# Two-layer hybrid encoder with top-2-of-8 experts: weights stored in tiles of one piece per partition, and two of twelve half loads of the few-token experts multiplied whole in plain fp32

## What is computed

```python
def swiglu(h, w1, w3, w2):
    return (jax.nn.silu(h @ w1) * (h @ w3)) @ w2

def moe_ffn(h, router, w1, w3, w2):
    ...
    logits = (t @ router).astype(jnp.float32)
    top_v, top_i = lax.top_k(logits, TOP_K)
    top_w = jax.nn.softmax(top_v, axis=-1)
    gates = jnp.sum(jax.nn.one_hot(top_i, N_EXPERTS, dtype=jnp.float32) * top_w[..., None], axis=1)
    out = jnp.zeros_like(t)
    for e in range(N_EXPERTS):
        out = out + gates[:, e:e + 1] * swiglu(t, w1[e], w3[e], w2[e])
```

## Time and profile before

| | before |
|---|---|
| median of 3 executions | 1627.55 us |
| lowest, highest | 1626.26, 1627.86 us |
| profiled execution, its own time | 1627.98 us |
| its span, first to last instruction | 1626.3 us |
| mean granted TensorE clock | 0.981 of 2.4 GHz |
| busy: PE, DVE, ACT, POOL | 1546.5, 1302.4, 1101.7, 30.5 us |
| mean DMA rate over the span | 283 GB/s |
| read from HBM | 457.96 MB |

### The profile page before, as it was taken

The page is one execution under the profiler, slowest core; times in us unless marked ns, Lnnn a source line. Parts: engine busy times, 40 slices in busy tenths (PEclk is TensorE's granted clock), DMA queues, the critical chain, the costliest instruction groups (busy, mean ns, idle before and its releaser), DMA issues.

```text
span 1626.3 us, 22748 instructions
## 1 busy us (share of the span) xinstructions
PE 1546.5 (95%) x8636; PEld 1311.1 (81%) x8636; DVE 1302.4 (80%) x1455; ACT 1101.7 (68%) x1299; POOL 30.5 (2%) x37
## 2 busy tenths in 40 slices
PE   7999999999999997999999988999998999898998
PEld 7999869999899984788888766888666788666786
DVE  4887745554688774789888999988999989999986
ACT  4775343333567523677777978878888778888785
POOL 3000000000000003000000000000000000000000
PEclk9999999999999998999999999999999999999999
DMA  9555356555455539699999999999999999999990
GB/s 261 179 162 181 105 185 195 185 186 182 138 174 159 179 112 381 252 357 356 362 346 351 371 371 374 392 359 357 367 375 372 392 356 344 382 364 383 390 362 26
DMA packets 231400, 460.55 MB, mean 283 GB/s; under 512 B 7434, under 2 KB 79478, under 8 KB 231286
## 3 DMA queue, kind: packets, MB, share of 16 engines
q1 hardware_dynamic: 230262, 457.22, 79.1%
q0 software_dynamic: 832, 1.74, 0.7%
q10 hardware_dynamic: 192, 0.08, 0.0%
HBM read 457.96 MB, written 1.05 MB: 282 GB/s over the span
## 4 chain that ended last, share of the span: by engine, by line
PE 71%; DVE 20%; ACT 6%; DMA 2%; issue 2%; ACTq 0%; SPq 0%; DVEq 0%
DVE w_lo L583 13%; PE bank L996 11%; PE bank L997 11%; PE bank L1000 11%; PE bank L739 8%; PE bank L740 8%; PE bank L741 8%; PE bank L784 3%; ACT w_hi L577 2%; PE bank L974 2%; DMA ring<-in_w_in 2%; PE bank L977 2%; PE bank L1031 1%; DVE w_lo L543 1%; ACT w_hi L535 1%
## 5 line engine op out<-in xcount | busy, mean ns | idle before, releaser
L583 DVE TENSOR_TENSOR w_lo<-arena,w_hi 128x1024 fp32r<-128x1024 f32 x486 | 574.0, 1220 | 54.6 <-ACT w_hi L577 46.7
L577 ACT ACTIVATE w_hi<-arena 128x1024 fp32r<-128x1024 f32 x492 | 503.9, 1056 | 114.1 <-PE bank L1000 88.6
L543 DVE TENSOR_TENSOR w_lo<-ring,w_hi 128x2048 fp32r<-128x2048 f32 x89 | 203.7, 2290 | 153.2 <-ACT w_hi L535 152.1
L739 PE MATMUL bank<-h_hi,w_hi 128*128 128x256 f32 x992 | 284.4, 287 | 4.3 <-DVE w_lo L543 2.6
L740 PE MATMUL bank<-h_lo,w_hi 128*128 128x256 f32 x992 | 282.1, 284 | 0.0
L741 PE MATMUL bank<-h_hi,w_lo 128*128 128x256 f32 x992 | 282.0, 284 | 0.0
L535 ACT ACTIVATE w_hi<-ring 128x2048 fp32r<-128x2048 f32 x89 | 170.2, 1914 | 123.1 <-PE bank L741 80.8
L583 DVE TENSOR_TENSOR w_lo<-ring,w_hi 128x1024 fp32r<-128x1024 f32 x180 | 213.3, 1220 | 19.4 <-ACT w_hi L577 16.9
L996 PE MATMUL bank<-w_hi,h_hi 128*128 128x512 f32 x560 | 224.2, 400 | 2.0 <-DVE h_lo L1912 2.0
L997 PE MATMUL bank<-w_hi,h_lo 128*128 128x512 f32 x560 | 218.8, 391 | 0.0
L577 ACT ACTIVATE w_hi<-ring 128x1024 fp32r<-128x1024 f32 x180 | 185.3, 1056 | 34.1 <-PE bank L1000 31.4
(11 more groups left out here) (281 smaller groups left out, 2111.6 us busy)
## 6 DMA issues: line engine op xcount, KB each, us to landing
arena<-in_moe_w SPq DMA_DIRECT2D x246, 1024.0 KB, 7.0
ring<-in_moe_w SPq DMA_DIRECT2D x90, 1024.0 KB, 6.9
ring<-in_ffn_w SPq DMA_DIRECT2D x33, 1024.0 KB, 5.3
ring<-in_w_gate SPq DMA_DIRECT2D x32, 1024.0 KB, 5.3
ring<-in_w_in SPq DMA_DIRECT2D x16, 1024.0 KB, 6.4
ring<-in_w_branch SPq DMA_DIRECT2D x8, 1024.0 KB, 4.9
ring<-in_w_out SPq DMA_DIRECT2D x8, 1024.0 KB, 4.9
x_tok<-in_x SPq DMA_DIRECT2D x2, 512.0 KB, 4.1
```

The lines of the kernel that those rows point to most:

```text
L543: nc.vector.tensor_tensor(w_lo[:, m % LO, :], raw, w_hi[:, m % HI, :].bitcast(F32), ALU.subtract)\
L577: nc.scalar.activation(half_hi[:, m % AHEAD, :], raw_of(n)[:, HALF * (m % 2):HALF * (m % 2) + HALF], ACT.Copy)\
L583: eng.tensor_tensor(half_lo[:, m % AHEAD, :], raw_of(m // 2)[:, HALF * (m % 2):HALF * (m % 2) + HALF], half_hi[:, m % AHEAD, :].bitcast(F3 ...
L739: pe.matmul(out_, a[0], b[0], start=start, stop=False)
```

## The change

Three things change. The ten large weights are stored in another order (`in_tiles`), in which the 1 MB of a unit or load is one stretch of memory with 8 KB per partition, so `drams` and `expert_drams` return it directly, and a DMA has one piece per partition. In a few-token expert, the third half of h1 and of h3 (q = 2, the k-tiles 4 and 5) is no longer split: `half_whole` multiplies the raw fp32 weight with an unsplit fp32 copy of the tokens (`h_few`, 64 columns), in two plain fp32 matmuls of 512 columns; ScalarE makes `h_few` once per such expert. And the splits are numbered by rank among the halves that are split, so buffers and the six-ahead distance count only these; SyncE waits for such a half to be used (`half_used`) instead of for its lo part. The `all_tokens` branch still splits every half.

```diff
--- before.py
+++ after.py
@@ -46,6 +46,9 @@
 AHEAD = 6
 SMALL = (2, 4, 6)
 FEW = 64
+WHOLE_Q = 2
+LAST_Q = 3
+FEW_K = 2 * WHOLE_Q - 4
...
+        self.whole = {self.first[(kind, i, 0)] + WHOLE_Q for kind in ("h1", "h3") for i in range(STEPS) if i // S_MOE in SMALL}
+        self.split = [m for m in range(self.halves) if m not in self.whole]
+        self.rank = {m: r for r, m in enumerate(self.split)}
...
+        h_few = mix(2, FEW)
...
-        def split_half_hi(m):
+        def split_half_hi(m, r, prior):
 
             n = m // 2
             nc.scalar.wait_ge(raw_loaded[n % RAW], 16 * (n // RAW + 1))
-            if m >= AHEAD:
-                nc.scalar.wait_ge(half_used, m - AHEAD + 1)
-            nc.scalar.activation(half_hi[:, m % AHEAD, :], raw_of(n)[:, HALF * (m % 2):HALF * (m % 2) + HALF], ACT.Copy)\
+            if prior is not None:
+                nc.scalar.wait_ge(half_used, prior + 1)
+            nc.scalar.activation(half_hi[:, r % AHEAD, :], raw_of(n)[:, HALF * (m % 2):HALF * (m % 2) + HALF], ACT.Copy)\
                 .then_inc(half_hi_done, 1)
 
-        def split_half_lo(eng, m):
-            eng.wait_ge(half_hi_done, m + 1)
-            eng.tensor_tensor(half_lo[:, m % AHEAD, :], raw_of(m // 2)[:, HALF * (m % 2):HALF * (m % 2) + HALF],
-                              half_hi[:, m % AHEAD, :].bitcast(F32), ALU.subtract)\
-                .then_inc(half_lo_pool if ex.by_pool(m) else half_lo_dve, 1)
+        def split_half_lo(eng, m, r, halves=1):
+            eng.wait_ge(half_hi_done, r + 1)
+            eng.tensor_tensor(half_lo[:, r % AHEAD, :], raw_of(m // 2)[:, HALF * (m % 2):HALF * (m % 2) + HALF],
+                              half_hi[:, r % AHEAD, :].bitcast(F32), ALU.subtract)\
+                .then_inc(half_lo_pool if ex.by_pool(m) else half_lo_dve, halves)
...
             if kind == "in":
                 _, l, w = key
-                return w_in[l].rearrange("(k p) c -> p k c", p=P)[:, :, IN_COL[w]:IN_COL[w] + US]
+                return w_in[l, 0, IN_COL[w] // US]
...
             if kind == "w2":
-                rows = MU * s + 2 * P * j
-                return w[at, rows:rows + 2 * P, :].rearrange("o (k p) d -> p (o k) d", p=P)
-            rows = D // 2 * j
-            return w[at, rows:rows + D // 2, MU * s:MU * s + MU].rearrange("o (k p) f -> p (o k) f", p=P)
+                return moe_w2[0, at, 2 * s + j, 0].rearrange("o p c -> p (o c)")
+            return {"h1": moe_w1, "h3": moe_w3}[kind][0, at, j, s].rearrange("o p c -> p (o c)")
...
                 j = n % RAW
                 if n >= RAW:
                     for m in (2 * (n - RAW), 2 * (n - RAW) + 1):
-                        wait_half_lo(sp, m)
+                        if m in ex.whole:
+                            sp.wait_ge(half_used, m + 1)
+                        else:
+                            wait_half_lo(sp, m)
...
-                src = expert_drams(key, expert)
-                sp.dma_start(raw_of(n).rearrange("p (k c) -> p k c", k=src.shape[1]), src).then_inc(raw_loaded[j], 16)
+                sp.dma_start(raw_of(n), expert_drams(key, expert)).then_inc(raw_loaded[j], 16)
...
             def half_few(m, outs, first, final):
 
-                pe.wait_ge(half_hi_done, m + 1)
-                w, wl = half_hi[:, m % AHEAD, :], half_lo[:, m % AHEAD, :]
+                r = ex.rank[m]
+                pe.wait_ge(half_hi_done, r + 1)
+                w, wl = half_hi[:, r % AHEAD, :], half_lo[:, r % AHEAD, :]
                 for x, (both, cols, dst) in enumerate(outs):
...
+            def half_whole(m, outs):
+                n = m // 2
+                pe.wait_ge(raw_loaded[n % RAW], 16 * (n // RAW + 1))
+                w = raw_of(n)[:, HALF * (m % 2):HALF * (m % 2) + HALF]
+                for whole, cols, dst in outs:
+                    last = pe.matmul(dst, whole, w[:, cols], start=False, stop=False, skip_group_check=True)
+                last.then_inc(half_used, 1)
             def inner_few(kind, i, toks, b):
                 for q in range(4):
+                    m = ex.first[(kind, i, 0)] + q
+                    if m in ex.whole:
+                        half_whole(m, [(h_few[:, k, :], slice(MU * k, MU * k + MU), bank[b][0:FEW, :]) for k in range(2)])
+                        continue
                     outs = [(h_hi[:, 2 * q + k, toks], slice(MU * k, MU * k + MU), bank[b][:, :]) for k in range(2)]
-                    half_few(ex.first[(kind, i, 0)] + q, outs, lambda x: q == 0 and x == 0, lambda x: q == 3 and x == 1)
+                    half_few(m, outs, lambda x: q == 0 and x == 0, lambda x: q == LAST_Q and x == 1)
...
             def next_hi(u):
+                if u in ex.rank and ex.rank[u] + AHEAD < len(ex.split):
+                    r = ex.rank[u] + AHEAD
+                    split_half_hi(ex.split[r], r, u)
+            def next_hi_all(u):
                 if u + AHEAD < ex.halves:
...
+                if e in SMALL and c == 1:
+                    fn(h_few, bank[b][:, :].rearrange("p (k n) -> p k n", k=4)[:, FEW_K:FEW_K + 2, 0:FEW], ACT.Copy)
...
             def next_lo(u):
-                m = u + AHEAD
-                if m < ex.halves and not ex.by_pool(m):
-                    split_half_lo(dve, m)
+                if u in ex.rank and ex.rank[u] + AHEAD < len(ex.split):
+                    r = ex.rank[u] + AHEAD
+                    split_half_lo(dve, ex.split[r], r, ex.split[r] - ex.split[r - 1])
...
+TILES = {"w_in": (D, US), "w_gate": (D, US), "w_branch": (US, D), "w_out": (US, D), "ffn_w1": (D, US), "ffn_w3": (D, US),
+         "ffn_w2": (US, D), "moe_w1": (D // 2, MU), "moe_w3": (D // 2, MU), "moe_w2": (2 * P, D)}
+def in_tiles(a, rows, cols):
+    lead, (r, c) = a.shape[:-2], a.shape[-2:]
+    n = len(lead)
+    a = a.reshape(*lead, r // rows, rows // P, P, c // cols, cols)
+    a = a.transpose(*range(n), n, n + 3, n + 2, n + 1, n + 4)
+    return a.reshape(*lead, r // rows, c // cols, P, rows // P * cols)
...
-        a = np.ascontiguousarray(inputs[name])
+        a = np.ascontiguousarray(in_tiles(inputs[name], *TILES[name]) if name in TILES else inputs[name])
```

More of the change, by code:

```diff
@@ L989, in outer_few, with half @@
                     half_few(ex.first[("w2", i, 0)] + c, outs, lambda x: first and c == 0, lambda x: final and c == 3)
[L991 to L994 removed]
+            def half(m, r, outs, first, final):
+                pe.wait_ge(half_hi_done, r + 1)
+                w, wl = half_hi[:, r % AHEAD, :], half_lo[:, r % AHEAD, :]
                 for x, (hi, lo, cols, dst) in enumerate(outs):
@@ L1007, in inner, with outer @@
                             for toks, b in tiles for k in range(2)]
-                    half(ex.first[(kind, i, 0)] + q, outs, lambda x: q == 0 and x % 2 == 0, lambda x: q == 3 and x % 2 == 1)
-            def outer(i, acts):
+                    m = ex.first[(kind, i, 0)] + q
+                    half(m, rank(m), outs, lambda x: q == 0 and x % 2 == 0, lambda x: q == 3 and x % 2 == 1)
+            def outer(i, acts, rank):
                 first, final = i % S_MOE == 0, i % S_MOE == S_MOE - 1
@@ L1014, in outer @@
                     outs = [(hi, lo, slice(512 * n, 512 * n + 512), bank[b + n][:, :]) for hi, lo, b in acts(c) for n in range(2)]
-                    half(ex.first[("w2", i, 0)] + c, outs, lambda x: first and c == 0, lambda x: final and c == 3)
+                    m = ex.first[("w2", i, 0)] + c
+                    half(m, rank(m), outs, lambda x: first and c == 0, lambda x: final and c == 3)
             def gather(e, c, b):
@@ L1117, in all_tokens @@
                     if i < STEPS:
-                        inner("h1", i, [(tiles[t], 4 + t) for t in range(TT)])
-                        inner("h3", i, [(tiles[t], 6 + t) for t in range(TT)])
+                        inner("h1", i, [(tiles[t], 4 + t) for t in range(TT)], int)
+                        inner("h3", i, [(tiles[t], 6 + t) for t in range(TT)], int)
                     if i >= 1:
```

42 lines of the change are left out of this document (19 added, 23 removed).

## The result

The changed kernel takes 1599.4 us (median of 4 runs, 1597.3 to 1600.5), the kernel before beside it 1626.9 us (1625.3 to 1627.9): a ratio of 0.983 (95% interval 0.982 to 0.985). That is 27.3 us less by the ratio, 27.5 by the medians. The forecast was 1601 us, in a range of 1590 to 1616.

What follows compares the result with a forecast made beforehand. TensorE was taken to bound regular experts and VectorE the few-token blocks. Whole halves (23.6 us) and larger pieces (2.7), with longer-held slots free, sum to 26.3: 1627.5 − 26.3 = 1601 us, range 1590 to 1616.

Steps and rivals of the forecast that it cites:

- the price of a whole half: On TensorE in few-token blocks: 1.79 us per whole half against 0.91 for a split one, 12.4 us more per block.
- part 1: Whole halves in the three few-token blocks: 7.4 us saved in the first, 8.1 in each other, 23.6 us in sum.
- part 3: One 8 KB piece per partition: first load 0.5, a later w_in 1.5, the experts' start 0.7, together 2.7 us.
- three signs of being wrong: TensorE waiting over 2 us for L1926, a whole half much other than 1.79 us, or ScalarE waiting for raw loads.
- the waits and couplings of 1.5 us per block: In few-token blocks: steps set by VectorE, 1.2 us, and remaining hand-over waits, allowed 1.5 us for all.
- my 97.1 us: TensorE's work in the first few-token block before the change, so a block can't be shorter than 97.1 + 12.4 = 109.5 us.
- Part 2: Raw weight slots are held longer, until TensorE has used them; still 9 us in hand, so no cost.
- 8 KB pieces at 415 GB/s: Rate of the weight loads in 8 KB pieces, bounded by 386 and 430 GB/s and taken as 415.
- Only half arrives: Rival: hand-overs between TensorE, VectorE and ScalarE cost 0.5 us more in each of 21 steps; 1612 us, chance 0.15.
- The saving in full: Rival: the plain matmuls fill TensorE's idle time without a price, VectorE's whole saving arrives; 1577 us, chance 0.07.
- Transfers cap it: Rival: the blocks' 373 GB/s is already the most served, so blocks can't shrink; 1625 us, chance 0.05.
- Slower by large pieces: Rival: 8 KB pieces are served below 370 GB/s, so every expert step waits for loads; 1643 us, chance 0.08.

Runs made afterwards that it cites:

- e5: The changed kernel with the whole halves' stationary operand 128 columns wide (upper 64 zeros) instead of 64: 1584.3 us, ratio 0.974 to the kernel before.
- e1: The changed kernel with no half whole and no h_few copy, only the new weight layout: 1618.8 us, ratio 0.996 to the kernel before.
- e2: The changed kernel with its whole halves, but all weights laid out and loaded as before: 1606.0 us, ratio 0.988 to the kernel before.
- e4: The changed kernel with only h1's half whole, 7 per block: 1598.2 us, ratio 0.983 to the kernel before.
- e3: The changed kernel with only h3's half whole, 7 per block: 1592.9 us, ratio 0.980 to the kernel before.
- e11: The changed kernel with only the experts' weights laid out as before (2 and 4 KB pieces): 1601.6 us, ratio 0.984 to the kernel before.
- e12: The changed kernel with w_in alone in the new layout, every other weight as before: 1601.2 us, ratio 0.984 to the kernel before.

## Why the prediction was right, and where its terms were off

The forecast was 1.6 us above the result, and its mechanism is what happened: TensorE becomes the bound of the blocks. But two terms of the sum were clearly mis-sized, the price of a whole half and the start. By the traces part 1 brought 2.0 us less than forecast and part 3 brought 3.3 more; that they nearly offset each other is luck.

- *The counts* hold: L590 624 times on VectorE, 168 records of L991, no wait of L584 for a transfer in a block, TensorE idle for 0 us per block at clock 1.00 (forecast: under 4). The steps are longer than the forecast's 13.9 to 15.5 us, 14.4 to 16.5, and of its three signs of being wrong one came: "if a whole half takes much other than 1.79 us".
- *Part 1, 23.6 us*: 21.6 by the trace, 19.5 (16.9 to 22.3) by the time of the whole halves alone. In the blocks 6.6, 7.5 and 7.5 us arrived for 7.4, 8.1 and 8.1.
- *The term that failed in it: "A whole half is thus 2 × 0.867 + 0.06 = 1.79", with "the 64 stationary columns change nothing that I can price".* It is 2.09, +1.18 instead of +0.88, 4.2 us per block. The price was right for the 128 columns of the rows that it came from (there 1.73, in e5) and was carried over to a width that no row showed.
- *What made up for it*: the waits and couplings of 1.5 us per block came to none, and TensorE's other work was less than my 97.1 us: a block that was 118.4 is now 118.4 - 6.6 = 111.8, which less 14 × 1.18 leaves 95.3. Together 4.2 - 1.5 - 1.8 = 0.9 us more than the forecast 111.0; measured 0.8. The 95.3 is a remainder, not counted row by row.
- *Clock*: full clock in all three blocks, as forecast; they are now equally long.
- *Part 2, no cost*: right. The landing in the experts went from 7.0 to 7.5 us, SyncE waits for L991 in a block, and ScalarE never waits for a load there, even with the old pieces at 8.7.
- *Part 3, 2.7 us*: too small. 6.7 (4.4 to 9.1) by the layout alone, 6.0 in the changed kernel's trace ahead of the first product. "First load 0.5" came to 0.16: SyncE issues faster, but the landing is nearly as late. "A later w_in 1.5" came to 2.8 by 40 us. The experts' start, 0.7, came to 1.0. The rest, 1.6, is the stretch at half clock behind the experts' first matmul, which every kernel with the experts' weights as before has and none with them in tiles; the forecast didn't count it at all. "In the blocks the layout is worth nothing by itself": right (e1, e2).
- *8 KB pieces at 415 GB/s*: the transfers of 940 to 1000 us, in 40 slices of 1.5 us, are among the fullest:

```profile
GB/s 421 426 431 415 410 410 431 344 426 426 426 426 421 426 410 399 415 333 350 393 333 393 415 431 399 355 382 404 350 322 404 437 415 415 426 426 431 426 426 437
```

  The first seven have 410 to 431, 421 in the mean, and 421 is also the page's fullest slice of 40 us (395 with the old pieces, in e2). So 415 was 6 too low. The estimate of 430 from the Trainium skill's page DMA: Bandwidth & Descriptors, section Why small descriptors are slow, is 9 too high; the trace comes to within 2% of it.
- *The rivals.* Only half arrives: no, TensorE waits for none of the hand-overs here; it does when h1's half alone is whole (e4's first step). The saving in full: no, TensorE has no idle time left to fill. Transfers cap it: no, 384 to 386 GB/s over whole blocks where 373 had been taken. The rule of the Trainium skill's page DMA: Bandwidth & Descriptors, section Where 436 GB/s comes from, by which the HBM's share of a core (about 358 GB/s) binds for loads, doesn't hold in these rows, where this core is alone. Slower by large pieces: no.
- *What I didn't see*: that 14 is past the best number. The forecast's own terms had it: VectorE's loop 13.9 us against TensorE's 15.3 in four steps says that TensorE is the longer path there, and that fewer whole halves would be faster. It only asked whether the change was faster, not where its balance lay.
- *The span of the forecast*: its lower end, 1592, isn't what its terms give. Without the coupling loss and with 4.7 us from part 3 they give 1627.5 - 28.1 - 4.7 = 1594.7. Nothing hangs on it here.

## What to carry to other kernels

When work is moved from one engine to another, work out both paths as functions of how much is moved, and stop where they cross: here half of the whole halves gave 33 us with the layout, all of them 27. Keep the place in mind too, as e3 and e4 differ by 5 us with the same number. Keep the stationary operands of neighbouring matmuls equally wide, padding with zeros if need be, before believing a price per matmul. And a larger piece per transfer pays where a transfer is waited for (one weight at the start), not where the queue is full but early.

## What the runs showed of the hardware that was not expected

- A stationary operand of 64 columns between ones of 128 costs 0.36 us per visit, at the two changes of width: its first weight load and the next 128-wide one are no longer hidden. The 64-wide load itself is shorter (0.14 us for 0.19).
- Pieces of 2 and 4 KB are served at a flat 392 to 395 GB/s in the blocks, in slices of 40 us (e2, e11, e12); pieces of 8 KB reach 421.
- SyncE's issue of three 1 MB loads takes 1.39 us in pieces of 8 KB and 4.37 in pieces of 1 KB, and the first of them lands 0.16 us earlier for it.
- The granted clock behind the experts' first matmul follows the layout of the experts' weights: 1.00 over 4 us in ten kernels with 8 KB pieces, 0.50 to 0.69 in four with 2 and 4 KB, worth 1.6 to 2.5 us. Why isn't shown.
